# Two-block transformer kernel: the first modulation in four groups of 32 array columns, and the scan tables spread over the next projections too

## The reference, cut to what matters

```python
silu_c = jax.nn.silu(c)            # (1, 2048)
silu_cc = jax.nn.silu(c_ctx)       # (2048,)
for l in range(DEPTH):
    shift, scale, gate = jnp.split(silu_c @ w_mod[l] + b_mod[l], 3, axis=-1)
    shift_c, scale_c, gate_c = jnp.split(silu_cc @ w_mod[l] + b_mod[l], 3, axis=-1)
    n = rms_norm(h, pre_norm_g[l]) * (1.0 + scale[:, None]) + shift[:, None]
    nc = rms_norm(hc, pre_norm_g[l]) * (1.0 + scale_c) + shift_c
    p = jnp.split(n @ w_in[l], split_points, axis=-1)
    ...
# second block, in the scan over L tokens:
lam_bar = jnp.exp(lam * dt)        # its powers need cos and sin of step * phase
```

## Time and profile before

| what | value |
|---|---|
| median of three runs | 3088.93 us (3087.02 to 3090.65) |
| span of the profiled execution | 3086.5 us |
| PE busy / PEld busy | 2915.4 / 2360.9 us (94% / 76%) |
| DVE / ACT / POOL busy | 1935.7 / 1165.1 / 347.8 us |
| moved by DMA | 484.79 MB, 157 GB/s over the span |

### The profile page before, as it was taken

One profiled execution on the slowest core, in us unless ns is written; L12 is line 12 of the kernel. 1 busy time (PEld: TensorE's weight loads), 2 busy tenths in 40 slices (PEclk: granted clock), 3 DMA queues, 4 the chain that ended last, 5 costly groups with the idle time before them and its releaser, 6 DMA issues. The chain is left out here.

```text
span 3086.5 us, 40408 instructions
## 1 busy us (share of the span) xinstructions
PE 2915.4 (94%) x15557; PEld 2360.9 (76%) x15557; DVE 1935.7 (63%) x3401; ACT 1165.1 (38%) x1870; POOL 347.8 (11%) x317
## 2 busy tenths in 40 slices
PE   7989899999989997999999999989999999999998
PEld 2447687787768776768777778765789999999887
DVE  3237777676777867462545657885866666666444
ACT  3233332323323235242433443233254444444443
POOL 5760000000000000000000004542400000000000
PEclk9989999999999998999999999985899999999999
DMA  9846245353344565432333444420344555555554
GB/s 337 281 143 229 99 142 188 110 167 113 106 150 162 196 220 201 143 111 95 123 109 110 146 157 152 133 87 22 100 150 151 191 182 181 185 189 181 194 191 154
DMA packets 154593, 484.79 MB, mean 157 GB/s; under 512 B 17168, under 2 KB 18192, under 8 KB 153232
## 3 DMA queue, kind: packets, MB, share of 16 engines
q1 hardware_dynamic: 144576, 448.33, 42.8%
q10 hardware_dynamic: 9824, 33.88, 2.9%
HBM read 469.03 MB, written 13.11 MB: 156 GB/s over the span
## 5 line engine op out<-in xcount | busy, mean ns | idle before, releaser
L1493 DVE TENSOR_TENSOR split_weights<-common,split_weights 128x1024 fp32r<-128x1024 f32 x644 | 797.5, 1247 | 618.8 <-ACT split_weights L2217 563.6
L2217 ACT ACTIVATE split_weights<-common 128x1024 fp32r<-128x1024 f32 x644 | 671.1, 1052 | 801.5 <-PE bank L1169 764.9
L1167 PE MATMUL bank<-split_weights,features 128*128 128x512 f32 x1920 | 804.2, 419 | 51.7 <-DVE split_weights L1493 18.6
L1169 PE MATMUL bank<-split_weights,features 128*128 128x512 f32 x1920 | 757.9, 395 | 0.0
L1168 PE MATMUL bank<-split_weights,features 128*128 128x512 f32 x1920 | 756.9, 394 | 0.0
L1167 PEld LDWEIGHTS bank<-split_weights,features 128*128 128x128 f32 x1920 | 366.3, 191 | 163.4 <-issue 49.8
L1169 PEld LDWEIGHTS bank<-split_weights,features 128*128 128x128 f32 x1920 | 365.2, 190 | 80.2
L1168 PEld LDWEIGHTS bank<-split_weights,features 128*128 128x128 f32 x1920 | 366.5, 191 | 78.1 <-issue 11.3
L1167 PE MATMUL bank<-ffn_input_split,split_weights 128*128 128x256 f32 (+1 forms) x1376 | 389.1, 283 | 0.8 <-issue 0.8
L1616 DVE CUSTOM_DVE_ANT_0 common<-first_block_work,common 128x512 f32<-128x512 f32 x448 | 336.1, 750 | 85.2 <-DMA first_block_work<-w_mod_cols 67.4
L1169 PE MATMUL bank<-ffn_input_split,split_weights 128*128 128x256 f32 (+1 forms) x1376 | 388.2, 282 | 0.0
(11 more groups left out here) (295 smaller groups left out, 3395.5 us busy)
## 6 DMA issues: line engine op xcount, KB each, us to landing
common<-w_in SPq DMA_DIRECT2D x260, 512.0 KB, 3.3
common<-w_up SPq DMA_DIRECT2D x172, 512.0 KB, 4.3
first_block_work<-w_mod_cols SPq DMA_DIRECT2D x256, 256.0 KB, 3.7
common<-w_out SPq DMA_DIRECT2D x104, 512.0 KB, 3.3
common<-w_down SPq DMA_DIRECT2D x84, 512.0 KB, 3.3
old_stream<-w_mod SPq DMA_DIRECT2D x64, 512.0 KB, 5.1
trig<-common ACTq DMA_DIRECT2D x32, 272.0 KB, 4.7
second_block_work<-trig SPq DMA_DIRECT2D x32, 272.0 KB, 3.0
```

The source lines that it names most:

```text
L1167: e.matmul(out_ap, xs[0], ws[0], start=first, stop=False)
L1169: return e.matmul(out_ap, xs[0], ws[1], start=False, stop=last)
L1493: e.tensor_tensor(lo, raw, hi.bitcast(F32), ALU.subtract).then_inc(*low_done.tick(("lo", m)))
L2217: e.activation(split_slots[:, 0, i, 0:words], raw_slots[:, m % RAW, 0:words], ACT.Copy).then_inc(*high_done.tick(("high", m)))
```

## The change

It has two parts.

**Column groups.** The silu vectors now stand in blocks of 32 columns (`silu_wide`), of which two are filled and 30 are zero. The matmul for input block kk goes to array columns 32 (kk mod 4) to 32 (kk mod 4) + 31 and writes bank rows of the same numbers. So each group of columns sums four of the 16 input blocks, and the four partial sums stand in rows 0 and 1, 32 and 33, 64 and 65, 96 and 97. VectorE copies all 128 rows. Instead of the transpose there is a matmul with the copied rows as weights (128 x 128) and a selection matrix `pick` of two columns as the moving operand (ones at those rows); it turns and adds in one step. `pick` is summed out of the identity by one VectorE instruction, the zeros are written by one GpSimd memset, and the silu vectors lie in `rows_buf[0]`.

**Tables.** The stage advances the tables by one at pieces whose number leaves 0 or 2 when divided by 5, not at every second one. The run of tables at its end is gone. From the last round's products on, one table is made at every 8 clocks, and the rest (`tables_done`) ahead of the attention of the first group. `trig_w`, the scratch of the angles, moves from the shared room to a place of its own, since that room's upper part is now used at the same time.

```diff
+GROUP = 32
+GROUPS_OF_COLUMNS = P // GROUP
+TABLE_EVERY = 8
...
+        if self.tables_beside and self.tables and self.clock % TABLE_EVERY == 0:
+            self.advance(self.tables)
...
-                    if i or c:
-                        step += 1
-                        if step % 2:
-                            self.do("table_angles", step // 2)
-                            if step > 2:
-                                self.do("table", step // 2 - 1)
+                    if (i or c) and done % 5 in (0, 2):
+                        self.advance(self.tables)
...
-        for j in range(step // 2, SJ):
-            self.do("table", j - 1)
-            self.do("table_angles", j)
-        self.do("table", SJ - 1)
-        self.do("tables_end")
+        self.tables_beside = True
         for piece in pieces:
             self.first_products(*piece)
+
+    def scan_tables(self):
+        for j in range(SJ):
+            self.do("table_angles", j)
+            if j:
+                self.do("table", j - 1)
+            yield
+        self.do("table", SJ - 1)
+
+    def tables_done(self):
+        while self.tables:
+            self.advance(self.tables)
+        self.do("tables_end")
...
+            if l == 0 and place == 0:
+                self.tables_done()
             self.side_work.append(self.attention(l, g, kind, kvh, qtiles))
...
-    silu_c = W.two(KT, 2)
+    silu_wide = rows_buf[0].rearrange("p (k n) -> p k n", n=GROUP)
+    silu_c = silu_wide[:, :, 0:2]
...
-                done = e.matmul(bank[0:2, :], silu_c[:, kk, :], mod_slots[:, w % MOD_SLOTS, k * CH:(k + 1) * CH],
-                                start=kk == 0, stop=kk == KT - 1)
+                group = GROUP * (kk % GROUPS_OF_COLUMNS)
+                done = e.matmul(bank[group:group + GROUP, :], silu_wide[:, kk, :], mod_slots[:, w % MOD_SLOTS, k * CH:(k + 1) * CH],
+                                start=kk < GROUPS_OF_COLUMNS, stop=kk >= KT - GROUPS_OF_COLUMNS, tile_position=(0, group))
...
-                done = e.transpose(tb[:, 2 * j:2 * j + 2], rows[:, j * P:(j + 1) * P], ident[0:2, 0:2])
+                done = e.matmul(tb[:, 2 * j:2 * j + 2], scratch[:, j * P:(j + 1) * P], pick, start=True, stop=True)
...
+            e.tensor_reduce(pick, ident.rearrange("p (g c) -> p c g", c=GROUP)[:, 0:2, :], AX.X, ALU.add).then_inc(
+                *modulation_scaled.tick(("picked",)))
...
-            e.tensor_copy(scratch[0:2, :], banks[6 + c // 4][0:2, :]).then_inc(
+            e.tensor_copy(scratch, banks[6 + c // 4][:, :]).then_inc(
...
+            for s, n in seen.new(at("silu_zeroed")):
+                e.wait_ge(s, n)
...
+            e.memset(silu_wide, 0.0).then_inc(*silu_cleared.tick(("silu_zeroed",)))
```

More of the change, by code:

```diff
@@ L242, in __init__ @@
         self.feature_set = None
+        self.tables, self.tables_beside = [], False
         self.group_ends, self.mixed_end, self.feature_end = {}, {}, {}
@@ L360, in first_stage @@
         self.feature_set = ("normed", 0)
-        step, self.mod_loaded, done = 0, 0, 0
+        self.tables.append(self.scan_tables())
+        self.mod_loaded, done = 0, 0
         q, k = self.projections, self.projections + 1
@@ L979, in build @@
     feat = feat_r[:, :].rearrange("p (s k t) -> p s k t", s=2, k=KT)
-    work_words = NT * D + NCONST1 + 3 * CH + KT * 2 + MODRING * CH + 2 * CH + 3 * HD
+    work_words = NT * D + NCONST1 + 3 * CH + MODRING * CH + 2 * CH + 3 * HD + 2 * T2
     work_held, work_t = tensor("first_block_work", work_words)
@@ L993, in build @@
     qk_g = W.two(2, HD)
+    trig_w = W.two(2, T2)
     H = Room(h_t_words, KT * T2)
@@ L1012, in build @@
     ssm.update(r=ssm_r, ph=ssm_ph, cr=ssm_cr, ci=ssm_ci)
-    steps_row, trig_x, trig_w = rows_buf[1][:, 0:T2], [B.two(2, T2) for _ in range(2)], B.two(2, T2)
+    steps_row, trig_x = rows_buf[1][:, 0:T2], [B.two(2, T2) for _ in range(2)]
     trig_out = [B.two(2, T2) for _ in range(2)]
+    assert B.at <= 5 * CH
     work_held.__exit__(None, None, None)
@@ L1060, in build @@
     half_b = small.one(ST)
+    pick = small.one(2)
     def flat(ap):
@@ L1184, in mod_products @@
                 kk = KP * kg + k
-                done = e.matmul(bank[0:2, :], silu_c[:, kk, :], mod_slots[:, w % MOD_SLOTS, k * CH:(k + 1) * CH],
-                                start=kk == 0, stop=kk == KT - 1)
+                group = GROUP * (kk % GROUPS_OF_COLUMNS)
+                done = e.matmul(bank[group:group + GROUP, :], silu_wide[:, kk, :], mod_slots[:, w % MOD_SLOTS, k * CH:(k + 1) * CH],
+                                start=kk < GROUPS_OF_COLUMNS, stop=kk >= KT - GROUPS_OF_COLUMNS, tile_position=(0, group))
             done.then_inc(*modulation_done.tick(("mod_used", w), *[("mod_done", c)] * (kg == KT // KP - 1)))
         def mod_turn(c):
-            tb, rows = banks[6 + c // 4], scratch[0:2, :]
-            for s, n in seen.new(at("mod_sums", c), tb.claim("mod_turn", c)):
+            tb = banks[6 + c // 4]
+            for s, n in seen.new(at("mod_sums", c), at("picked"), tb.claim("mod_turn", c)):
                 e.wait_ge(s, n)
             for j in range(4):
-                done = e.transpose(tb[:, 2 * j:2 * j + 2], rows[:, j * P:(j + 1) * P], ident[0:2, 0:2])
+                done = e.matmul(tb[:, 2 * j:2 * j + 2], scratch[:, j * P:(j + 1) * P], pick, start=True, stop=True)
             names = [("mod_turned", c)] + ([("scratch", 0)] if c == MOD_FIRST - 1 else [])
@@ L2661, in scalar_program @@
                 tasks[name](*args)
-    powers_done, tables_reduced, scan_pairs, zeros_made = (
-        signal(n) for n in ("powers_done", "tables_reduced", "scan_pairs", "zeros_made"))
+    powers_done, tables_reduced, scan_pairs, zeros_made, silu_cleared = (
+        signal(n) for n in ("powers_done", "tables_reduced", "scan_pairs", "zeros_made", "silu_cleared"))
     def gpsimd_program(e):
```

## The result

| | before | after |
|---|---|---|
| median (lowest to highest), beside each other on one chip | 3089.79 us (3087.02 to 3091.39, 4 runs) | 3037.18 us (3031.33 to 3039.22, 4 runs) |
| ratio, 95% interval | | 0.9833 (0.9815 to 0.9851) |
| span of the profiled execution | 3086.5 us | 3036.6 us |

The forecast was 3039 us with a range of 3023 to 3060. The same kernel, run again beside the later experiments, gave 3039.0 us and a ratio of 0.9847 (0.9831 to 0.9863).

A forecast was written before the change was run, and what follows sets the result against it. The prediction took TensorE to bound the modulation rounds. From a span of 3086.5 us, -42 for start and rounds, -9 and +1 for tables gave 3036.5; with 2.4 from span to median, 3039 us, range 3023 to 3060.

The forecast's parts named there:

- Bound before: Middle modulation rounds of the old kernel: TensorE busy 45.80 of 45.80 us, so it bounds them; a round lasts 45.9 us.
- Four groups together: Modulation matmuls: four on different column groups run at once in 1.06 us, a round's 32 in 8.5 us; chance 0.68.
- No overlap: Rival for the modulation matmuls: column groups do not run together, rounds stay at 45.9 us; 3083 us, chance 0.10.
- weights wait for the array: Rival: weights cannot load during matmuls on the same rows, a record costs 0.71 us instead of 0.43; 3149 us, chance 0.05.
- two at a time: Rival: only neighbouring modulation matmuls overlap, TensorE's round is 37.5 us and binds; 3047 us, chance 0.13.
- TensorE's round of 29 us: TensorE's work per changed round: 8.5 modulation, 16.2 products, 2 turns, 1.4 joints and 1 features, 29 us.
- Clock: Rival: pauses inside rounds lower TensorE's clock, costing 2 to 4 us for one 3 us pause; only widens the range.
- What is late next: Changed rounds: TensorE 29 us, GpSimd 30 and DMA 30 to 37 wait for each other; 36 us a round taken.
- Start and first round: Second chunk's addition at 46.7 us instead of 54.72, then a first round of 37.5 us.
- The tables: Behind the stage: removing the table run brings back 9 us of stand and clock; function table loads cost 1 us.
- I expect nothing to be given back: After the stage: the same steps begin sooner with DMA far from full, so the whole gain stays.
- The sum: Whole kernel: -42 to the last addition, -9 and +1 for tables, -50 us; span 3036.5, median 2.4 above it.

The follow-up runs named there:

- two_groups: The changed kernel with neighbouring modulation matmuls alternating between only two column groups instead of four; 3042.85 us, ratio 0.9857 to the kernel before.
- half_bytes: The changed kernel loading only the first 512 columns of each `w_mod` piece and using them for both halves; 3032.23 us, ratio 0.9824 to the kernel before.
- few_angles: The changed kernel with angles computed for the first two tables only, sines and stores kept, other values left out; ratio 0.9796 to the kernel before.
- groups_only: The changed kernel's column groups with the old placing of the tables; 3054.13 us, ratio 0.9894 to the kernel before.
- dve_angles: The changed kernel with the tables' angles computed on VectorE instead of GpSimd, at the same places; ratio 0.9841 to the kernel before.

## Why the prediction was right, and where it was not

**Bound before: right.** The rounds were TensorE's; sparing it 78.5 us of modulation moved the last addition by 46.1.

**Four groups together: right, the size off.** The term was 0.53 us a pass, read from two score matmuls that share the columns; it is 0.43. A round's 32 matmuls cost 6.9 us by their passes, and 7.6 from start to start with the step to the next line, not 8.5. The turn was put at 1 us and takes 0.98. "No overlap" and "weights wait for the array" fell with the window at 139.93; two_groups shows what "two at a time" would have been, 3043 us against the 3047 worked out.

**TensorE's round of 29 us: 3.7 too low.** The work is 6.9 + 16.2 + 2 = 25.1 us. With the steps between lines, for which the sum had 1.4, and a mean clock of 0.95, where 1.00 was assumed, TensorE is busy 28.6. The clock is the rival *Clock* in small: behind the idle 2.43 us at 91.81 the products start 0.43 us apart until 95.2, at half clock:

```profile
91.90:95.20 3.30, 3.30 (x8) 2.33 (x9) 1.62 (x4) 2.13 (x5) 0.00 (x0) 0.50 1.02 408
```

That is 1.65 us of the round (half of 3.3), a little under the 2 to 4 that were reckoned for a pause of 3 us, and it isn't hidden beside the DMA. To the 28.6 come 4.1 us of idle time at the joints, for which the sum had 1.

**"What is late next": the step that failed in size and in cause.** Rounds 2 and 3 were put at 36 us, near the DMA's upper end of 37. They took 32.7 and 31.8. The upper end was the old round's share times its length; in the round of 32.7 us the same engines moved 394 GB/s, so it was no bound. half_bytes then shows that the DMA does not set the rounds: with a share of 0.75 and 0.58 they last as long. What binds is TensorE with its joints, the features' chain and the copy ahead of the turn, and few_angles shows that GpSimd's tables lengthen both (rounds of 30.2 and 29.1 without them). The prediction had GpSimd's 30 us in its list, but took DMA for the later one. Its sign, a DMA share over 0.95 in the middle rounds, came for round 2 (1.02) and not for round 3 (0.81), and shows nothing either way.

**Start and first round: 48.37 and 39.2 us, against 46.7 and 37.5.** The first term took only the matmuls' time for the second chunk (and its parts, 39.2 + 4.3 + 1 + 2, make 46.5). But the line of the modulation has 2.6 us of waits for `w_mod` in all, and half_bytes got 4.4 us from the bytes. The first product came 12.0 us behind the addition, not 10; TensorE waited 7.40 us for VectorE's split. Together 3.4 us too good, against 7.5 us too bad in rounds 2 and 3: -46.1, not -42.

**The tables: -9 us and +1 forecast, nothing measured on their own.** The stand went as forecast (10.7 us at group 96). "I expect nothing to be given back" failed: 11.5 us went back by group 120. The sentence behind it, that 8 clocks of three products are 5.4 us and cover GpSimd's 4.72, has two faults. In the first products two groups of matmuls count three clocks, so 8 clocks are 5.3 groups or 3.6 us; and a table behind the stage took up to 7.0 us on GpSimd. Of the four more function table loads, for which the sum had 1 us, one stands inside the 3.62 us stand. So the prediction's own sign of being wrong, tables that hold ScalarE in the projections, came true beside a right total. On the other side the spread of the tables is what let the rounds fall to 32 us (groups_only: 40.5), and that worth the sum had booked under the column groups.

**The sum.** -50 forecast, -49.9 in the traces, +2.4 from span to median assumed, and the median is 0.6 over the span of the profiled run. The mechanism of the larger term was right; that the total fits to 2 us is luck. Up to the last addition the kernel gained 4 us more than forecast (46.1, not 42). From there to group 204 it gained 0.6 us where the tables were to bring 8. And 3.2 us more came behind group 204, which no step named and which lie within the 3.8 us that two executions of this kernel differ there.

## What to carry to other kernels

- Narrow float32 matmuls over the same rows cost little more than a quarter when neighbours in the queue go to four different groups of 32 columns (16 records in 1.92 us instead of 7.03), and the summing turn costs about a microsecond. Alternate the groups matmul by matmul.
- When the bound of a loop falls, count again what each other engine does per round; here GpSimd's eight tables, 38 us, would have kept a third of the gain (groups_only). And look at what its work does to the joints: even the 6.4 tables that are left lengthen a round of 32.7 us by some 2.5 (few_angles).
- A DMA share of 1.0 doesn't show that a stretch waits for the DMA. Look at what ends the idle time of the engine that matters; and a wait that is moved in in-order queues often stands up again at the next place where something depends on the same producer.

## What the runs showed of the hardware that was not expected

- Four float32 matmuls on four column groups take 0.43 us a pass of 512 columns, as one does, and the weight loads run beside them on the same rows.
- With one group used four times in a row, 16 records took 12 slots. The fifth matmul, on another column group, started with the third, ahead of the fourth, which was queued for a busy group.
- GpSimd's work beside it slows a VectorE addition of 128 x 512 from 0.69 to 1.47 us (few_angles against the kernel after). GpSimd's angles of one table took 7.0 us where most take 4.3 to 5.3; that VectorE caused it is not shown. The same angles take 1.9 us on VectorE (dve_angles).
- The DMA engines move 394 GB/s through a whole round of TensorE work at a share of 1.02, and the round is no shorter when half of the stage's weight bytes are left out (half_bytes).
- Behind an idle 2.4 us of TensorE its granted clock was 0.50 for the next 3.3 us, and matmuls that start 0.23 us apart started 0.43 us apart (kernel after, 91.90 to 95.20).
